# A decoder layer with expert retrieval on one core: PSUM copy for the dots, merged one-hots, a second top-k block in the query stage, and score tiles in three banks

## The chip, the cores and the metric

One core of a Trainium2 chip runs the whole layer. The metric is device time in microseconds (us) of one execution, lower is better. The times are those of the kernel before and of the changed kernel on such a core, and the trace is one profiled execution of each.

## What is computed

One sequence of 1024 tokens of width 1024 in float32 goes through a projection, retention and sliding-window attention, an output projection, a layer norm, and then an expert layer (PEER), whose result is normalised again. The change lies in the expert layer:

```python
q = (xt @ w_pq).reshape(T, H, 2, PEER_HALF)              # H = 8 heads
s = jnp.einsum('thpd,hpkd->thpk', q, sub_keys)           # 128 keys a side
s1, i1 = lax.top_k(s[:, :, 0], K)                        # K = 16
s2, i2 = lax.top_k(s[:, :, 1], K)
cand = (s1[..., :, None] + s2[..., None, :]).reshape(T, H, K * K)
top_s, pos = lax.top_k(cand, K)
idx = jnp.take_along_axis(cand_idx, pos, axis=-1)        # of 16384 experts
g = jax.nn.softmax(top_s, axis=-1)
a = gelu(einsum('cd,ced->ce', xb, u_tab[idx])) * g       # the dots
y = einsum('ce,ced->cd', a, v_tab[idx])
```

## The kernel before, in words

The tokens are eight blocks of 128. Five stages follow one another, each an own block of instructions for the engines, with a barrier between them: `project`, `attend`, `score` (the query stage), `experts_in` and `experts_out`. Float32 products of large matrices are done as three passes over a high and a low part (hi times hi, hi times lo, lo times hi).

The query stage (`score`, from L797 on) has a turn for each of 8 heads: 96 matmuls of 512 columns give the queries, 16 small ones the scores. ScalarE takes the first half of the queries and scores out of PSUM and VectorE the second (`query`, `scores`). The scores of blocks 1 to 7 go to memory; those of block 0 stay (`s_cp`), and VectorE finds their top 16 at the end of the turn of heads 0 to 6: `side` for either side, `pairs` for the sums, and `names` for two heads at a time. Head 7 of block 0 is left to the beginning of `experts_in`.

The expert layer treats the blocks in two ways. For blocks 2 to 7 (768 tokens, `DB` = 6) it multiplies the tokens by all 16384 experts: `experts_in` computes z = u h, 128 tiles of 128 experts, and beside it a dense matrix of gates from one-hots; `experts_out` multiplies gelu(z) times the gates by v. For blocks 0 and 1 (`GB` = 2) it gathers rows: POOL fetches the chosen row of u for 128 tokens with an indirect DMA (`gather`, L1191), and VectorE forms its dot product with the block's tokens (`dot`, L1259), which `h_own` holds in SBUF. There are 2 x 128 = 256 such gathers and dots. They share a ring of three row tiles (`RING` = 3, two gathers ahead): the gather of row i+2 waits until dot i-1 is done (`row_used`).

`experts_in` is laid out by hand in 8 turns of 32 slots. In each slot TensorE does half a tile of z (`z_half`, L1084 to L1086: 24 matmuls of 384 columns). All engines walk through the slots in order, and within a slot in this order:

- TensorE: half a tile, then the gate matmuls (`gates`, 4 small ones, L1094) of the slot before. A tile needs `u_lo` of POOL, and a z bank that ScalarE has read.
- ScalarE: at even slots `u_hi` of the next tile, then the copy of z out of PSUM (L1153) and the store of a whole tile, `scale_hot` (L1125), `take_gates` (L1136), and every 8 steps the store of 2 MB of gates (L1141).
- POOL: at even slots `u_lo` of the next tile (L793), which waits for `u_hi`; then the gathers of the slot. A gather that waits keeps all later work of POOL waiting, `u_lo` too.
- VectorE: the one-hots (`make_hot`, L1248: two instructions of 512 elements a step, which read `near`, a PSUM tile with the numbers 0 to 127, and `iT`), then a piece of the next block's top-k (`top_piece`: three pieces for a head, one for `names`), then the dots of the slot (`own_rows`, from `PER_TURN`).
- SP: u tiles as `u_lo` frees their buffers, the scores for top-k, and in the last turn the first loads of `experts_out` (L1056 z, L1061 and L1069 gates, L1064 v).

Turn s finds the top-k of block s+1, and turns 2 to 7 make the gates of blocks 2 to 7: 32 steps in each, one in a slot, and in turn 7 the same 32 in 21 slots. A step is one make_hot, one scale_hot, one gates and one take_gates, on two sets of buffers in turn. At slot 0 of turns 2 to 7 TensorE transposes the block's `found` and waits for `found_in` (L1107), which VectorE raises at the end of the turn before (L1299). PER_TURN, the dots in the eight turns, is 28, 40, 27, 27, 27, 27, 27, 53.

## Time and profile before

| | before |
|---|---|
| median of 3 runs | 3114.03 us (3112.42 to 3116.70) |
| the profiled execution | 3114.11 us, of which the trace spans 3112.3 us |
| TensorE matmul busy | 2979.0 us, 96% |
| VectorE busy | 2450.3 us, 79% |
| ScalarE, POOL busy | 1191.8 us (38%), 1159.7 us (37%) |
| mean granted TensorE clock | 0.984 |
| chain that ended last | PE 32%, all others 1% or less (the chain covers the last stage) |

The profiler's page says how busy each engine is and which groups of instructions are costliest. A matmul's busy time there overlaps with its neighbour's (they are pipelined), so the time of a run of matmuls is read from their starts in the timeline. A `start us, us` row of the timeline is: start, duration, engine, line, operation, written tile <- read tiles, shapes, and in brackets how long the engine sat idle before and what released it. "SPq", "ACTq" rows are issues of DMAs. The spans of the 8 turns of `experts_in` are found in the timeline as the start of every 768th matmul of L1084 to L1086.

### The profile page before, as it was taken

The page shows a single profiled execution, that of the slowest core. Times are in us where ns is not written, and L with a number is a line of the kernel's source. Part 1 is how long each engine was busy: PE and PEld are TensorE (multiplying, and loading weights), DVE is VectorE, ACT ScalarE, POOL GpSimd, SP SyncE. Part 2 cuts the span into 40 slices and gives each one's busy share as a digit, 9 for nine tenths or more (in the row PEclk, how much of TensorE's full clock was granted, in tenths as well). Part 3 has the DMA queues.
Part 4 walks back from the last instruction along what each step waited for, and adds up shares of the span by engine and source line. Part 5 has one row for each costly group of instructions (what it writes and reads, how often), then busy time and mean ns, then how long its engine had stood idle before and what let it go on. Part 6 is the DMA issues. An engine that isn't in the chain of part 4 may idle for free. (4 is left out here: it accounts for less than half of the span.)

```text
span 3112.3 us, 42565 instructions
## 1 busy us (share of the span) xinstructions
PE 2979.0 (96%) x15866; PEld 2686.6 (86%) x15866; DVE 2450.3 (79%) x4511; ACT 1191.8 (38%) x2213; POOL 1159.7 (37%) x750
## 2 busy tenths in 40 slices
PE   8996998999999999999999999869999999999998
PEld 6886886888999999999999998858888888888887
DVE  4214775455999999999999986569989898999898
ACT  2112332111222466666666656523333333333331
POOL 3222211002656544443444445524434333344331
PEclk9998998999999999999999999989999999999999
DMA  4223222223777666666667677889988888888882
GB/s 172 79 88 132 93 96 82 76 91 114 240 251 255 224 229 239 224 239 243 243 236 240 235 268 280 281 287 314 327 287 307 287 309 307 280 305 297 297 306 78
DMA packets 294024, 695.57 MB, mean 223 GB/s; under 512 B 20432, under 2 KB 136528, under 8 KB 290640
## 3 DMA queue, kind: packets, MB, share of 16 engines
q1 hardware_dynamic: 190928, 316.66, 30.6%
q0 software_dynamic: 73728, 268.47, 25.0%
q10 hardware_dynamic: 29184, 108.01, 9.0%
q8 instruction: 113, 1.85, 0.2%
q14 instruction: 71, 0.58, 0.1%
HBM read 565.13 MB, written 127.93 MB: 223 GB/s over the span
## 5 line engine op out<-in xcount | busy, mean ns | idle before, releaser
L1084 PE MATMUL z_ps<-hT_hi,u_hi 128*128 128x384 f32 x2048 | 703.2, 343 | 18.2 <-POOL u_lo L793 12.7
L1085 PE MATMUL z_ps<-hT_lo,u_hi 128*128 128x384 f32 x2048 | 687.5, 336 | 0.0
L1086 PE MATMUL z_ps<-hT_hi,u_lo 128*128 128x384 f32 x2048 | 687.1, 335 | 0.0
L1393 PE MATMUL y_ps<-v_hi,a_hi 128*128 128x512 f32 x1536 | 600.2, 391 | 24.4 <-DVE y L1521 11.6
L1394 PE MATMUL y_ps<-v_lo,a_hi 128*128 128x512 f32 x1536 | 599.5, 390 | 0.0
L1395 PE MATMUL y_ps<-v_hi,a_lo 128*128 128x512 f32 x1536 | 599.2, 390 | 0.0
L793 POOL TENSOR_TENSOR u_lo<-u_raw,u_hi 128x1024 fp32r<-128x1024 f32 x128 | 315.4, 2464 | 618.2 <-ACT u_hi L789 617.3
L1453 POOL DMA_INDIRECT v_rows<-in_v,room x192 | 286.1, 1490 | 437.8 <-DVE y L1500 414.3
L1084 PEld LDWEIGHTS z_ps<-hT_hi,u_hi 128*128 128x128 f32 x2048 | 387.6, 189 | 20.9 <-POOL u_lo L793 15.3
L1085 PEld LDWEIGHTS z_ps<-hT_lo,u_hi 128*128 128x128 f32 x2048 | 387.6, 189 | 0.0
L1086 PEld LDWEIGHTS z_ps<-hT_hi,u_lo 128*128 128x128 f32 x2048 | 386.6, 189 | 0.0
L1393 PEld LDWEIGHTS y_ps<-v_hi,a_hi 128*128 128x128 f32 x1536 | 289.5, 188 | 85.9 <-issue 12.0
L1394 PEld LDWEIGHTS y_ps<-v_lo,a_hi 128*128 128x128 f32 x1536 | 289.7, 189 | 60.3
L1395 PEld LDWEIGHTS y_ps<-v_hi,a_lo 128*128 128x128 f32 x1536 | 289.5, 188 | 60.2
L1521 DVE TENSOR_TENSOR y<-y_ps,y 128x512 f32<-128x512 f32 x384 | 255.7, 687 | 80.1 <-PE y_ps L1395 77.0
L1259 DVE CUSTOM_DVE_ANT_0 u_rows<-u_rows,h_own 128x1024 f32<-128x1024 f32 x170 | 276.9, 1629 | 46.5 <-DMA u_rows<-in_u,room 34.3
L1153 ACT ACTIVATE z_sb<-z_ps 128x384 f32<-128x384 f32 x256 | 125.8, 491 | 484.1 <-PE z_ps L1086 484.1
L1248 DVE TENSOR_TENSOR hot<-near,iT 128x512 f32<-128x512 f32 x384 | 246.1, 683 | 47.9 <-PE g_ps L1094 47.0
L1125 ACT ACTIVATE hot_g<-hot,gT 128x128 f32<-128x128 f32 x768 | 244.7, 392 | 94.2 <-DVE hot L1248 73.5
L1191 POOL DMA_INDIRECT u_rows<-in_u,room x170 | 208.6, 1227 | 156.3 <-DVE room L1259 132.3
L1500 DVE SCALAR_TENSOR_TENSOR y<-v_rows,a_rows,y 128x1024 f32<-128x1024 f32 x192 | 243.0, 1280 | 4.0 <-DMA v_rows<-in_v,room 3.8
L1421 ACT ACTIVATE v_hi<-room 128x1024 fp32r<-128x1024 f32 x128 | 135.5, 1059 | 276.6 <-DMA room<-in_v 268.9
(189 smaller groups left out, 4818.7 us busy)
## 6 DMA issues: line engine op xcount, KB each, us to landing
u_raw<-in_uT SPq DMA_DIRECT2D x128, 512.0 KB, 3.7
room<-in_v SPq DMA_DIRECT2D x128, 512.0 KB, 6.3
z<-z_sb ACTq DMA_DIRECT2D x128, 384.0 KB, 5.2
gates<-g_sb ACTq DMA_DIRECT2D x24, 2048.0 KB, 8.8
room<-z SPq DMA_DIRECT2D x16, 1536.0 KB, 9.0
z_in<-z SPq DMA_DIRECT2D x16, 1536.0 KB, 8.2
g_in<-gates SPq DMA_DIRECT2D x16, 1536.0 KB, 17.5
room<-gates SPq DMA_DIRECT2D x15, 1536.0 KB, 17.9
```

Of the source, the lines that this page charges most:

```text
L793: self.nc.gpsimd.tensor_tensor(self.u_lo[e][:], self.u_raw[e][:], self.u_hi[e][:].bitcast(F32), ALU.subtract).then_inc(self.u_lo_in[e], 1)
L1084: nc.tensor.matmul(o, u_hi[e][:, k], hT_hi[:, k, cols], start=(k == 0), stop=False)
L1085: nc.tensor.matmul(o, u_hi[e][:, k], hT_lo[:, k, cols], start=False, stop=False)
L1086: last = nc.tensor.matmul(o, u_lo[e][:, k], hT_hi[:, k, cols], start=False, stop=(k == KT - 1))
L1125: last = nc.scalar.activation(hot1_g[g][:, t], hot1[g][:, t], ACT.Copy, scale=gT[:, t0 + t:t0 + t + 1])
L1248: last = nc.vector.tensor_tensor(hot[g][:], bc(iota_ps, 1, 4), bc(iT[:, side, t0:t0 + 4], 2, NK), ALU.is_equal)
L1259: nc.vector.tensor_tensor_reduce(rows_in[r][:], rows_in[r][:], h_own[b][:], 1.0, 0.0, ALU.mult, ALU.add, ahead.z_rows[:, b, slot:slot + 1] ...
L1393: nc.tensor.matmul(o, ah, v_hi[p][:, i, c], start=(i == 0), stop=False)
L1394: nc.tensor.matmul(o, ah, v_lo[p][:, i, c], start=False, stop=False)
L1395: last = nc.tensor.matmul(o, al, v_hi[p][:, i, c], start=False, stop=(i == GROUP - 1))
L1453: nc.gpsimd.indirect_dma_start(out=rows_in[i % RING][:], out_offset=None, in_=d["v"].rearrange("a b c -> (a b) c"), in_offset=bass.Indirec ...
L1521: nc.vector.tensor_tensor(y[:, GB + s, c], y_ps[n % 8][:], y[:, GB + s, c], ALU.add).then_inc(y_read, 1)
```

## The change

Four things change in the expert layer; `UB` is a new constant, equal to `GB`, so that the parts of the diff that treat `UB` > `GB` do nothing here.

1. Dots: one `h_own` of SBUF in place of two, copied by VectorE at the block's first dot into a PSUM tile `h_ps` of two banks, and the dots read that copy.
2. One-hots: the two instructions of `make_hot` become one that writes both (1024 elements).
3. Top-k: in the query stage VectorE finds the top-k of blocks 0 and 1 for heads 0 to 6, one turn later than before. All evacuations of PSUM there go to ScalarE. Head 7 of both blocks, and their gates, come at the beginning of `experts_in`; turn s then treats block s+2, so that turns 6 and 7 have no top-k. The buffers of top-k are doubled. The gathers begin at slot 4 in place of 2 and the dots at slot 6 in place of 4; the dots of the turns are 24, 34, 27, 27, 27, 27, 45, 45.
4. z: a tile's 768 columns are cut into 512 and 256 in place of 384 and 384. The 256 of two tiles share a bank (`z_rest`), so that z needs three banks in place of four and `h_ps` finds room. The second half of a tile now also waits until ScalarE has read the other half of that bank, which is the tile before.

```diff
+UB = 2
+ZB = TB - UB
+ZT = ZB * P
...
-                def query(h, p):
-                    v.wait_ge(q_done, 4 * h + 2 * p + 2)
-                    nc.vector.tensor_copy(qT[p][:, HT:T], q_ps[p][1][:]).then_inc(q_dve, 1)
...
+                def search(h, b):
+                    for p in range(2):
+                        tk.side(link, p, b, h, tk.s_cp[:, b, p])
+                    tk.pairs(link, b, h)
+                    if h % 2:
+                        tk.names(link, b, h // 2)
 
                 def turn(h):
-                    last = h == PH - 1
-                    query(h, 0)
-                    if not last:
+                    if h:
+                        search(h - 1, 0)
+                    if h < PH - 1:
                         split_w(h + 1, 0)
-                    scores(h, 0)
-                    query(h, 1)
-                    if not last:
+                    if h:
+                        search(h - 1, 1)
+                    if h < PH - 1:
                         split_w(h + 1, 1)
-                    scores(h, 1)
-                    v.wait_ge(s_act, 2 * h + 2)
...
+                    v.wait_ge(s_act, 4 * h + 4)
...
-    HT = DT // 2
+    CUT = ZT - 2 * P
...
-    PER_TURN = [28, 40, 27, 27, 27, 27, 27, 53]
+    PER_TURN = [24, 34, 27, 27, 27, 27, 45, 45]
...
-        z_ps = [[bank(f"z_ps{e}{a}") for a in range(2)] for e in range(2)]
+        z_first, z_rest = [bank(f"z_first{e}") for e in range(2)], bank("z_rest")
+        z_ps = [[z_first[e][:, 0:CUT], z_rest[:, e * 2 * P:(e + 1) * 2 * P]] for e in range(2)]
+        h_ps = ctx.enter_context(nc.psum_tensor("h_ps", [P, D], F32))
...
+                def z_half(tile, a):
+
+                    e, i = tile % 2, tile // 2
                     if a == 0:
...
+                        pe.wait_ge(u_lo_in[e], i + 1)
+                        wait(pe, z_read[e], 2 * i)
+                    else:
+                        wait(pe, z_read[1 - e], 2 * ((tile + 1) // 2))
+                    cols = slice(UB * P, UB * P + CUT) if a == 0 else slice(UB * P + CUT, T)
...
+                        if s == 0 and k in (1, 3):
+                            act.wait_ge(gaps, k // 2 + 1)
+                            tk.exp(k // 2).then_inc(exps, 1)
...
-                        if s == 0 and k == 2:
+                        if s == 0 and k == 4:
                             for i in range(EARLY):
                                 gather(i)
...
-                    for hot, side in ((hot2, 1), (hot1, 0)):
-                        last = nc.vector.tensor_tensor(hot[g][:], bc(iota_ps, 1, 4), bc(iT[:, side, t0:t0 + 4], 2, NK),
-                                                       ALU.is_equal)
-                    last.then_inc(hot_in[g], 1)
+                    nc.vector.tensor_tensor(hot[g][:], bc(bc(iota_ps, 1, 4), 1, 2), bc(iT[:, :, t0:t0 + 4], 3, NK),
+                                            ALU.is_equal).then_inc(hot_in[g], 1)
...
+                        v.wait_ge(h_here, 16 * (i // (PH * TOPK) + 1))
+                        link(nc.vector.tensor_copy(h_ps[:], h_own[:]))
+                        nc.vector.engine_nop().then_inc(h_taken, 1)
+                    nc.vector.tensor_tensor_reduce(rows_in[r][:], rows_in[r][:], h_ps[:], 1.0, 0.0, ALU.mult, ALU.add,
                                                    ahead.z_rows[:, b, slot:slot + 1]).then_inc(row_used, 1)
...
+                for b in range(2):
+                    for p in range(2):
+                        tk.side(link, p, b, PH - 1, tk.s_cp[:, b, p])
+                    tk.pairs(link, b, PH - 1)
+                    tk.gaps(b).then_inc(gaps, 1)
+                for b in range(2):
+                    tk.names(link, b, PH // 2 - 1)
+                    v.wait_ge(exps, b + 1)
+                    tk.gates(link, b)
+                    keep_picked(b)
```

## Rows read from the trace of the kernel before

**Rows 1.** Windows: span, busy per engine, clock, DMA share, GB/s; stages and turns.

```profile
531.10:743.80 212.70, 207.21 (x1024) 175.30 (x1024) 93.80 (x249) 34.26 (x48) 2.40 (x1) 0.98 0.25 78
743.80:879.10 135.30, 135.26 (x769) 135.29 (x770) 127.89 (x314) 32.65 (x49) 77.61 (x45) 0.98 0.71 236
879.10:1023.00 143.90, 135.15 (x769) 132.91 (x768) 133.54 (x308) 33.05 (x49) 91.72 (x55) 1.00 0.78 252
1023.00:1189.60 166.60, 163.77 (x1028) 163.45 (x1028) 154.63 (x354) 100.76 (x209) 74.65 (x45) 0.99 0.65 225
1189.60:1351.70 162.10, 162.10 (x1031) 162.07 (x1029) 151.40 (x349) 101.90 (x210) 72.17 (x43) 1.00 0.68 237
...
1837.90:2026.50 188.60, 171.15 (x1029) 167.98 (x1028) 114.79 (x176) 105.14 (x215) 96.94 (x66) 0.96 0.81 287
...
2037.50:3101.30 1063.80, 1050.36 (x4608) 868.26 (x4608) 948.40 (x1185) 340.87 (x504) 391.02 (x262) 0.99 0.84 288
```

**Rows 2.** Waits of TensorE: total us, times, longest.

```profile
PE z_ps L1084 <- POOL u_lo L793: 12.7, 8, 4.0
...
PE g_ps L1094 <- ACT hot_g L1125: 8.9, 4, 3.6
...
PE g_ps L1094 <- ACT g_sb L1136: 4.5, 5, 1.1
PE g_ps L1107 <- DVEq L1299: 2.8, 1, 2.8
```

**Rows 3.** Timeline of TensorE: each row starts 24 matmuls after its partner.

```profile
236.14 0.39 PE L167 MATMUL pp<-w_hi,x_hi 128*128 128x512 f32 x1
...
241.58 0.28 PE L167 MATMUL pp<-w_hi,x_hi 128*128 128x256 f32 x1
...
244.46 0.28 PE L167 MATMUL pp<-w_hi,x_hi 128*128 128x256 f32 x1
...
999.67 0.33 PE L1084 MATMUL z_ps<-hT_hi,u_hi 128*128 128x384 f32 x1
...
1003.83 0.33 PE L1084 MATMUL z_ps<-hT_hi,u_hi 128*128 128x384 f32 x1
```

**Rows 4.** One line's instructions on VectorE: count, duration ns min/median/max.

```profile
L1259 DVE CUSTOM_DVE_ANT_0 u_rows<-u_rows,h_own x170: 1209/1226/3845, 773.1 to 2028.9; 128x1024 f32<-128x1024 f32 x170
...
L1248 DVE TENSOR_TENSOR hot<-near,iT x384: 673/681/693, 1032.4 to 1978.1; 128x512 f32<-128x512 f32 x192
...
L1508 DVE TENSOR_TENSOR z_in<-z_in,g_in x96: 680/686/696, 2071.8 to 3068.4; 128x512 f32<-128x512 f32 x96
```

**Rows 5.** Timeline of VectorE and POOL at the beginning of experts_in (from 743.8).

```profile
750.13 0.29 DVE L742 TENSOR_TENSOR gap<-best 128x128 f32<-128x128 f32 x1
...
755.81 0.29 DVE L767 TENSOR_REDUCE gap_sum<-gap_e 128x8 f32<-128x128 f32 x1 [1.37 <-ACT gap_e L763]
...
759.37 0.29 DVE L724 MAX8 top<-s_in 128x8 f32<-128x128 f32 x1
...
773.21 3.42 POOL L793 TENSOR_TENSOR u_lo<-u_raw,u_hi 128x1024 fp32r<-128x1024 f32 x1 [1.59 <-ACT u_hi L789]
...
774.30 2.37 DVE L749 TENSOR_SCALAR ab<-pos 128x32 uint32<-128x32 uint32 x1
```

**Rows 6.** Timeline of three engines at the beginning of turn 7.

```profile
1839.42 0.33 ACTq L1141 DMA_DIRECT2D gates<-g_sb  x1
...
1845.61 0.94 POOL L1191 DMA_INDIRECT u_rows<-in_u,room  x1 [0.30 <-issue]
...
1854.33 1.22 DVE L1259 CUSTOM_DVE_ANT_0 u_rows<-u_rows,h_own 128x1024 f32<-128x1024 f32 x1 [4.78 <-DMA u_rows<-in_u,room]
```

**Rows 7.** Groups of VectorE in turn 7 (1837.9 to 2026.5): busy, mean, idle before.

```profile
L1259 DVE CUSTOM_DVE_ANT_0 u_rows<-u_rows,h_own 128x1024 f32<-128x1024 f32 x34 | 50.0, 1469 | 35.5 <-DMA u_rows<-in_u,room 34.3
...
L1259 DVE CUSTOM_DVE_ANT_0 room<-room,h_own 128x1024 f32<-128x1024 f32 x18 | 22.7, 1263 | 17.8 <-DMA room<-in_u,room 17.1
```

**Rows 8.** DMA issues of turn 7: count, us from issue to landing.

```profile
u_rows<-in_u,room POOLq DMA_INDIRECT x34, 6.4
```

More of the change, by code:

```diff
@@ L895, in turn @@
                     last = isinstance(h, int) and h == PH - 1
-                    query(h, 0)
+                    query(h, 0, 0)
+                    query(h, 0, 1)
                     if not last:
                         split_w(h + 1, 0)
-                    query(h, 1)
-                    scores(h, 0)
+                    query(h, 1, 0)
+                    for a in range(2):
+                        scores(h, 0, a)
+                    query(h, 1, 1)
                     if not last:
@@ L1149, in _ @@
-                        act.wait_ge(z_done[e], 2 * (2 * m + j) + a + 1)
+                        tile, a = s * SLOTS // 2 + k // 2, k % 2
+                        e, i = tile % 2, tile // 2
+                        if a == 0 and tile < NK - 1:
+                            split_u(tile + 1)
+                        act.wait_ge(z_done[e], 2 * i + a + 1)
                         if a == 0:
-                            wait(act, z_stored[e], 16 * (2 * m + j))
-                        nc.scalar.activation(z_sb[e][:, a * HT:(a + 1) * HT], z_ps[e][a][:, 0:HT],
-                                             ACT.Copy).then_inc(z_read[e], 1)
+                            wait(act, z_stored[e], 16 * i)
@@ L1161, in _ @@
-                        if s < TB - 1 and k == SLOTS - 2:
-                            act.wait_ge(gaps, s + 2)
-                            tk.exp().then_inc(exps, 1)
+                            act.wait_ge(z_read[e], 2 * i + 2)
+                            act.dma_start(d["z"][tile], z_sb[e][:]).then_inc(z_stored[e], 16)
+                        if s == 0 and k in (1, 3):
+                            act.wait_ge(gaps, k // 2 + 1)
+                            tk.exp(k // 2).then_inc(exps, 1)
@@ L1164, in _ @@
+                        if s < TB - 2 and k == SLOTS - 2:
+                            act.wait_ge(gaps, s + 3)
+                            tk.exp(s + 2).then_inc(exps, 1)
+                        if UB > GB and s == TB - 2 and k == SLOTS - 6:
+                            act.wait_ge(row_used, 2 * PH * TOPK)
+                            nc.scalar.activation(kept[:, 2], ahead.z_rows[:, GB], ACT.Gelu).then_inc(late_gelu, 1)
                         for step in steps_at(s, k):
@@ L1291, in _ @@
                             dot(i)
+                        if UB > GB and s == TB - 2 and k == SLOTS - 2:
+                            v.wait_ge(late_gelu, 1)
+                            link(nc.vector.tensor_tensor(kept[:, 2], kept[:, 2], ahead.picked_g[:, GB], ALU.mult))
+                            nc.vector.engine_nop().then_inc(found_in, 1)
                         if s == TB - 1:
-                            for t in range(DB):
+                            for t in range(ZB):
                                 if PRODUCTS_AT[t] == k:
```

308 lines of the change are left out of this document (152 added, 156 removed).

## The prediction

> **What bounds the kernel now.** I read the page first: TensorE is busy 96% of the span. So the only time to be had, as long as TensorE's own work stays the same, is the time in which it stands still or is slowed. Then the windows, one for the query stage, one for each turn of `experts_in` and one for `experts_out` [rows 1]. The turns are the place to look. Turns 3 to 6 take 162.1 us each (one row stands for four), with TensorE busy for all of it: 162.1 is what a turn with 32 gate steps costs when nothing stalls. A turn without gates needs 32 halves of 4.16 us, 133.1 us: 24 matmuls start in 1003.83 - 999.67 = 4.16 us [rows 3]. Against these two floors stand turn 0 with 135.3 (+2.2), turn 1 with 143.9 (+10.8), turn 2 with 166.6 (+4.5) and turn 7 with 188.6 (+26.5) [rows 1]. That is 44 us in all, and the waits of TensorE name their owners: `u_lo` of POOL 12.7 us, the scaled one-hots of ScalarE 8.9, the reading of gates 4.5, `found_in` of VectorE 2.8 [rows 2]. They add up to less than 44 because the wait is followed by a stretch of less than the full clock (mean grant 0.96 in turn 7, 0.99 to 1.00 in turns 2 and 3 [rows 1]), and small gaps inside a step aren't listed.
>
> Behind all of these owners stands VectorE, for two different reasons. In **turn 1** it is full: busy 133.5 us [rows 1], which is as much as TensorE's whole floor of 133.1. Its dots come late, POOL's next gather waits for them in the ring of three, and `u_lo` is queued behind that gather. Turn 2 then begins with the wait for the end of turn 1's top-k. In **turn 7** it isn't full (114.8 of 188.6 us [rows 1]); it sits before the dots and waits for rows: 34.3 + 17.1 us of the turn [rows 7]. A store of 2 MB of gates is issued at 1839.42, a gather at 1845.61, and the dot of that time's rows starts at 1854.33 after 4.78 us of idleness [rows 6]; the one-hots of the next slot stand behind this dot, and TensorE behind the one-hots. A row lands 6.4 us after its issue in the middle [rows 8]; with the dot of 1.3 us and about 1.3 us until POOL issues again, three rows go round in 9 us, 3.0 us a row. Turn 7 asks for 53 rows in 162.1 us, 3.06 us a row. So there is no reserve with which to make good what a burst of transfers costs.
>
> **z in 512 and 256 columns.** 24 matmuls of 512 columns take 241.58 - 236.14 = 5.44 us, 24 of 256 take 244.46 - 241.58 = 2.88 us [rows 3]. Together 8.32 us, as much as 2 x 4.16. Cost 0. Slots are now long and short, 5.44 and 2.88 (with a gate step of (162.1 - 133.1) / 32 = 0.9 us: 6.3 and 3.8). The new wait for `z_read` of the tile before has the long half between, 5.44 us, and stands in TensorE's queue in front of the short half and the gates; ScalarE copies z first thing in its slot, so I take 0, and price a miss under the rivals.
>
> **The dot reads PSUM.** Before, a dot takes 1.226 us in the middle but 3.845 at most [rows 4], and 1.63 in the mean of the page. The one-hots, of which one operand is in PSUM, never take more than 0.693 in 384 [rows 4]. The long ones fall on POOL's `u_lo`: a tensor_scalar of only 32 elements on VectorE took 2.37 at 774.30 while `u_lo` ran from 773.21, and `u_lo` itself took 3.42 [rows 5]. So I price the dot with `h_ps` at 1.23 + 0.08 for reading the sum: 0.4 x 256 = 100 us less on VectorE, of which only what falls into turns 1, 2 and 7 can show. No row shows this instruction with a PSUM operand. Bounds: 1.22 (its minimum, 1.209, is no better) and twice, 2.45. The nearest row is the one-hots', which read PSUM in 0.681 against 0.686 for two SBUF operands of the same size [rows 4], so I take the lower end. The page "SBUF — State Buffer" of the Trainium skill (section "SBUF: two separate sides") says that POOL and a VectorE instruction with two SBUF inputs take a shared pair of ports for a whole instruction each; the trace agrees, 3.845 is about 1.2 plus one `u_lo`. The page "VectorE: DVE Perf Modes" (section on the errata) speaks a little against the change: a PSUM source has a fixed part of 120 cycles against 58, which by its clock would be 0.065 us more a dot, 17 us of VectorE in all; the two rows of equal size don't show it. Two copies of 1024 elements into PSUM, about 1.3 us each, lie in VectorE's queue: under 3 us, covered. The top-k's own two-input instructions can still be held by `u_lo`; I keep 3 to 5 us a turn for them.
>
> **One-hots in one.** Two of 0.681 become one of about 1.23 (the dot's length for 1024 elements): 0.14 x 192 = 26 us less on VectorE, 0.8 us of each pair of slots. TensorE has no wait for it in turns 3 to 6. Cost 0, gain only inside turn 7.
>
> **Top-k of a second block in the query stage.** One head's search takes 750.42 - 743.9 = 6.5 us with `gap`, so 6.2; `names` for two heads ends 1.37 before 755.81, at 754.44, so 4.1 [rows 5]. VectorE is busy 93.8 us of the stage's 212.7 [rows 1]. A turn of a head is 207/8 = 26 us; an odd head's two searches take 2 x (6.2 + 4.1) = 20.6, an even head's 12.4, and the splits of w add 2.4 and the copy 0.3. That fits, and 32 evacuations of 512 elements (some 0.7 us each) have left for ScalarE, which is busy 34.3 us of 212.7 [rows 1]. Splits needed next come between the searches; ahead of the latest stand 10 us of searching and then about 11 us until TensorE needs it. At the stage's end two more copies of 0.6 us run one after the other ahead of the scores' store, which carries 6 blocks in place of 7: +0.5 us. I take +0.5.
>
> **Beginning of experts_in.** VectorE now does two last heads (13), two `names` (8.2), two times gates and the picked numbers (2 x 1.4): it reaches turn 0's first piece about 25 us after the start in place of 15.6 (759.37 - 743.8 [rows 5]). ScalarE's two waits for `gap` come at 10.5 and 18.8 us, when `gap` is there since 6.5 and 13. The gathers wait in POOL's queue ahead of `u_lo`. I follow them: six pieces bring VectorE to 38, `names` to 42, the copy and the first dot to 45; gather 3 waits for it until 45, gather 4 until 48, `u_lo` of tile 6 is then done at 51.5, and TensorE wants it at slot 12, 52 us. A tie: I take 0, and keep 0 to 10 us (each `u_lo` that holds a piece of top-k adds up to 2.4 to VectorE's lateness). VectorE then has 67 + 24 x 1.31 = 98 us of work in turn 0 (67: 8 x 6.2 + 4 x 4.1 and the gates), and catches up.
>
> **Turns 1 and 2.** Turn 1: 67 + 34 x 1.31 + 5 = 117 us against 133.1, in place of 133.5 busy plus waits. `u_lo` isn't held any more: 143.9 becomes 133.3, -10.6. The block of turn 2 has been searched in turn 0, so `found_in` is there and the slower clock behind the wait goes as well: 166.6 becomes 162.3, -4.3.
>
> **Turns 3 to 6.** VectorE falls from 151.4 to about 32 x 1.23 + 67 + 27 x 1.31 + 5 = 147; turn 6 has 45 dots and no top-k, 98. TensorE is on its floor already: 0.
>
> **Turn 7.** 45 rows in 162.1 us are 3.6 us a row, against 3.0 for the ring: a reserve of 0.6 x 8 rows = 5 us between two stores of gates (5.3 slots), which is what a burst takes (4.78 [rows 6]). The turn also begins without a rest of top-k. Of the 26.5 us I let remain what falls to the first burst and to the late loads of gates and v, where no gates slow the slots and rows are asked for every 3.0 us again: 8 us. So 188.6 becomes 170, -18.5. Bounds 0 and -26.5.
>
> **Sum.** +0.5 + 0 - 10.6 - 4.3 - 18.5 = -33 us. `experts_out` (1063.8 us [rows 1]) keeps its work and its loads; VectorE's last dot lies no longer behind the last z store, -1 us. Against the profiled execution, 3114.1 - 34 = 3080 us; that execution stands 0.1 us from the median, so the same holds for it. Own range of this case 3068 to 3090: turn 7 without any stall gives 3072, less the transition's microseconds, and 10 us at the beginning gives 3090.
>
> **Rivals.**
> (a) Turn 7's stalls belong to the transfers, not to the number of rows: DMA share 0.81 at 287 GB/s there against 0.68 and 237 in turn 3 [rows 1]. Each store of gates then still holds a row, whatever the reserve, and only turns 1 and 2 pay: 3114 - 15 = 3099. For it: half of VectorE's idleness is before few rows. Against it: turn 3 to 6 have the same stores and no stall.
> (b) The late beginning: VectorE, held by `u_lo` several times, comes 5 us later than counted, and each pair of slots from 12 to 20 loses 2 us: +10, 3090 with the rest as forecast, 3105 together with (a).
> (c) Slower: the dot on PSUM costs more. Price at 2.45: a turn of 3 to 5 needs 39 + 67 + 27 x 2.53 + 5 = 179 against 162.1, +17 in turns 3 to 5 and +12 in turn 2, turns 0 and 1 (153 and 158 us) +32, turn 7 still -18: about 3190. It turns to a loss where the dot passes (162 - 111) / 27 = 1.9 us, less 0.08. Only the row of the one-hots speaks against it.
> (d) Slower: the short slots. ScalarE's time in a gate step (four scalings of 0.39, 1.1 for the gates, 0.5 for z) no longer fits between long and short halves, in the turn with two steps in a slot above all, and TensorE waits 0.5 us in every second slot of turns 2 to 7: 96 x 0.5 = +48, net 3128. Against it: counted through a pair, ScalarE is ready 1 to 2 us early with one step, and just in time with two.
> (e) Nothing happens: all of the stalls move to another owner. 3110.
>
> **Chances.** Forecast 0.60, (a) 0.17, (b) 0.08, (c) 0.05, (d) 0.05, (e) 0.05. The predicted time is the forecast's. The range, 3068 to 3103, takes in the forecast, (a) and most of (b). A difference under 0.2% (6 us) can hardly be told from none: faster 0.86, within 0.2% 0.05, slower 0.09.
>
> **What would show it.** Windows by turn: turn 1 near 133, turn 2 near 162, turn 7 near 170. Durations of the dot: a maximum near 1.25 in place of 3.85. TensorE's waits: no `u_lo` in turn 1, no L1107's. Starts 24 matmuls apart: 5.44 and 2.88. I am wrong if the dot's median leaves 1.23, if turns 3 to 6 leave 162.1 (short slots), or if turn 0 leaves 135.

## The result and the profile after

The changed kernel took 3082.06 us, median of 4 runs (3081.89 to 3082.50), against 3114.53 us of the kernel before in the same session (4 runs, 3112.42 to 3116.70): a ratio of 0.9896, with a 95% interval of 0.9879 to 0.9913. The forecast was 3080. The profiled execution has a span of 3080.7 us, 31.6 less than the 3112.3 of before.

The windows come first again, cut at the first z matmul of each turn, so that they answer to [rows 1]. Columns: stretch and length, then busy us (and count) of PE, PEld, DVE, ACT and POOL, the granted clock, the DMA share and GB/s. The stretches are the query stage, turns 0, 1, 2, 3, 6 and 7 of `experts_in`, and `experts_out`.

```profile
529.90:741.80 211.90, 206.53 (x1025) 175.36 (x1025) 127.39 (x411) 50.88 (x80) 2.34 (x1) 0.98 0.23 74
741.80:882.70 140.90, 138.09 (x768) 121.38 (x769) 125.39 (x350) 32.47 (x50) 64.06 (x42) 0.97 0.61 214
882.70:1016.10 133.40, 133.40 (x770) 118.07 (x769) 113.16 (x294) 32.90 (x49) 70.89 (x50) 1.00 0.71 249
1016.10:1179.10 163.00, 163.00 (x1030) 147.08 (x1028) 138.91 (x314) 100.21 (x209) 67.01 (x44) 1.00 0.64 228
1179.10:1342.10 163.00, 163.00 (x1029) 147.05 (x1029) 139.97 (x317) 101.41 (x210) 66.24 (x43) 1.00 0.66 236
1668.10:1831.10 163.00, 163.00 (x1030) 147.07 (x1029) 94.85 (x131) 101.33 (x209) 81.29 (x62) 1.00 0.79 284
1831.10:1998.80 167.70, 164.84 (x1030) 147.89 (x1028) 93.15 (x127) 105.60 (x216) 77.18 (x59) 1.00 0.84 306
2006.20:3069.70 1063.50, 1050.18 (x4608) 868.00 (x4607) 947.70 (x1185) 339.36 (x503) 356.03 (x261) 0.99 0.84 288
```

Set against the forecast, stretch by stretch, in us. The times are differences of the starts of every 768th z matmul, so they have two decimals; the windows above round them. The last z matmul is counted to turn 7 with 0.34 us. `experts_out` is taken from its first matmul's start to its last one's end (the last window above begins 0.4 us late).

| stretch | before | after | change | forecast |
|---|---|---|---|---|
| stages ahead of the query stage | 531.1 | 530.2 | -0.9 | none |
| query stage, to the first z matmul | 212.7 | 211.5 | -1.2 | +0.5 |
| turn 0 | 135.24 | 140.94 | +5.7 | 0 (0 to +10) |
| turn 1 | 143.93 | 133.44 | -10.5 | -10.6 |
| turn 2 | 166.61 | 162.93 | -3.7 | -4.3 |
| turns 3 to 6 | 4 x 162.06 | 4 x 163.01 | +3.8 | 0 |
| turn 7 | 188.65 | 167.64 | -21.0 | -18.5 |
| last z matmul to first of `experts_out` | 10.98 | 7.02 | -4.0 | -1 |
| `experts_out` | 1063.8 | 1063.9 | +0.1 | 0 |

They add up to -31.7, the difference of the spans but for rounding. The sum of the forecast was -34, so the total is close, but three terms are off by 3 to 6 us each and offset one another. The experiments are about these.

TensorE's waits from 700 to 2100 us (engine and line that waits, what it waits for, total us, times, longest), which answer to [rows 2]; two of `experts_out` are left out:

```profile
PE y_ps L1443 <- DVE a_lo L1564: 7.1, 1, 7.1
PE z_first L1104 <- PEq L825: 5.1, 1, 5.1
PE z_first L1104 <- POOL u_lo L799: 4.5, 2, 2.8
...
PE g_ps L1114 <- ACT g_sb L1157: 1.0, 1, 1.0
```

`u_lo` has gone from 12.7 us in 8 waits to 4.5 in 2, the scaled one-hots (8.9) are off the list, and so is the wait behind the top-k at a turn's beginning (2.8).

The dots, one line's instructions (count, ns min/median/max, first and last start), which answer to [rows 4]:

```profile
L1285 DVE CUSTOM_DVE_ANT_0 u_rows<-u_rows,h_ps x170: 1209/1221/1224, 792.5 to 1999.3; 128x1024 f32<-128x1024 f32 x170
L1285 DVE CUSTOM_DVE_ANT_0 room<-room,h_ps x86: 1209/1221/1223, 789.6 to 2000.7; 128x1024 f32<-128x1024 f32 x86
```

The longest of 256 dots is 1.224 us, where it was 3.845. Rival (c), a dearer dot, is out with that. The first dot also starts 20 us later than before (789.6 against 769.2).

### The profile page after: what moved, and what is told of

Read it like the earlier page. It is cut to its first block and busy times, and to the rows that moved or that the text cites. A ratio compares the mean times of both kernels' runs of the same rounds, so it can differ in the third digit from the quotient of the medians.

```text
span 3080.7 us, 42384 instructions
## 1 busy us (share of the span) xinstructions
PE 2980.4 (97%) x15866; PEld 2565.9 (83%) x15866; DVE 2327.8 (76%) x4289; ACT 1204.8 (39%) x2245; POOL 1053.0 (34%) x750
## 5 line engine op out<-in xcount | busy, mean ns | idle before, releaser
L1443 PE MATMUL y_ps<-v_hi,a_hi 128*128 128x512 f32 x1536 | 600.1, 391 | 20.4 <-DVE y L1572 11.5
L1104 PE MATMUL z_first<-hT_hi,u_hi 128*128 128x512 f32 x1024 | 409.9, 400 | 9.5 <-PEq L825 5.1
L1106 PE MATMUL z_first<-hT_hi,u_lo 128*128 128x512 f32 x1024 | 401.3, 392 | 0.0
L1105 PE MATMUL z_first<-hT_lo,u_hi 128*128 128x512 f32 x1024 | 400.7, 391 | 0.0
L1273 DVE TENSOR_TENSOR hot<-near,iT 128x1024 f32<-128x1024 f32 x192 | 234.1, 1222 | 124.2 <-PE g_ps L1114 122.2
L1104 PE MATMUL z_rest<-hT_hi,u_hi 128*128 128x256 f32 x1024 | 297.0, 290 | 0.0
L1105 PE MATMUL z_rest<-hT_lo,u_hi 128*128 128x256 f32 x1024 | 289.7, 283 | 0.0
L1106 PE MATMUL z_rest<-hT_hi,u_lo 128*128 128x256 f32 x1024 | 289.6, 283 | 0.0
L1285 DVE CUSTOM_DVE_ANT_0 u_rows<-u_rows,h_ps 128x1024 f32<-128x1024 f32 x170 | 207.3, 1219 | 73.7 <-DMA u_rows<-in_u,room 62.0
L1104 PEld LDWEIGHTS z_first<-hT_hi,u_hi 128*128 128x128 f32 x1024 | 193.7, 189 | 46.4 <-issue 5.2
L1106 PEld LDWEIGHTS z_first<-hT_hi,u_lo 128*128 128x128 f32 x1024 | 193.3, 189 | 42.5
```

The costliest lines, as they stand in the source:

```text
L1104: nc.tensor.matmul(o, u_hi[e][:, k], hT_hi[:, k, cols], start=(k == 0), stop=False)
L1105: nc.tensor.matmul(o, u_hi[e][:, k], hT_lo[:, k, cols], start=False, stop=False)
L1106: last = nc.tensor.matmul(o, u_lo[e][:, k], hT_hi[:, k, cols], start=False, stop=(k == KT - 1))
L1273: nc.vector.tensor_tensor(hot[g][:], bc(bc(iota_ps, 1, 4), 1, 2), bc(iT[:, :, t0:t0 + 4], 3, NK), ALU.is_equal).then_inc(hot_in[g], 1)
L1443: nc.tensor.matmul(o, ah, v_hi[p][:, i, c], start=(i == 0), stop=False)
```

## The experiments

The stretches of all profiled executions stand together here; each run's edit and verdict follow. `transition` is the stretch between the last z matmul and the first of `experts_out`. Each span is of one execution.

| kernel | turn 0 | turn 1 | turn 2 | turn 3 | turn 6 | turn 7 | transition | span |
|---|---|---|---|---|---|---|---|---|
| before | 135.24 | 143.93 | 166.61 | 162.06 | 162.07 | 188.65 | 10.98 | 3112.3 |
| after | 140.94 | 133.44 | 162.93 | 163.03 | 163.01 | 167.64 | 7.02 | 3080.7 |
| after, dots on SBUF | 141.96 | 133.44 | 162.91 | 163.01 | 165.85 | 176.06 | 11.52 | 3097.6 |
| before, z split | 135.47 | 144.78 | 164.88 | 163.11 | 163.14 | 189.92 | 10.38 | 3113.8 |
| before, z split, PSUM dots | 135.49 | 133.44 | 163.08 | 163.16 | 163.18 | 179.97 | 6.57 | 3086.6 |
| after, 53 rows in turn 7 | 141.00 | 133.44 | 162.91 | 163.03 | 163.01 | 177.77 | 6.67 | 3088.7 |
| after, two one-hots | 141.79 | 133.44 | 163.06 | 163.15 | 163.10 | 169.07 | 6.59 | 3081.6 |
| after, u loads first | 141.73 | 133.44 | 162.92 | 163.02 | 163.03 | 168.40 | 6.29 | 3081.0 |
| after, 384/384 and iota in SBUF | 140.46 | 133.12 | 162.67 | 162.76 | 164.86 | 174.49 | 7.09 | 3086.4 |
| u loads first, ring of 4 | 141.70 | 133.44 | 162.94 | 163.03 | 163.03 | 164.71 | 6.25 | 3077.3 |
| the same, dots from slot 12 | 136.14 | 133.44 | 162.92 | 163.06 | 163.02 | 164.33 | 6.25 | 3072.1 |
| after, again | 140.88 | 133.44 | 162.91 | 163.02 | 163.02 | 167.15 | 7.01 | 3077.5 |

The stretches hardly scatter: turn 1 is 133.44 in every kernel with z split and its stall gone, and the changed kernel's turn 7 came out at 167.64 and 167.15. So differences of half a microsecond can be read from single executions in turns 1 to 5. In turns 0 and 7 something under 1 us isn't safe: the order of SP's loads alone moved turn 7 by 0.8 (experiment 6). Those of spans can't be read so finely: the stages ahead of the query stage, which no edit here touches, vary from 527.0 to 531.7.

**1. Is it the place of the dot's operand?** The changed kernel, whose dots read the block from SBUF again, one tile for each of the two blocks; the copy into PSUM is still made. To find room, one small tile moves into free space of another, and one that nothing uses here goes.

```diff
-        h_own = sb("h_own", [P, D])
+        h_own = [sb(f"h_own{b}", [P, D]) for b in range(2)]
...
-                    nc.vector.tensor_tensor_reduce(rows_in[r][:], rows_in[r][:], h_ps[:], 1.0, 0.0, ALU.mult, ALU.add,
+                    nc.vector.tensor_tensor_reduce(rows_in[r][:], rows_in[r][:], h_own[b][:], 1.0, 0.0, ALU.mult, ALU.add,
```

> The changed kernel with one thing undone: the dots read the block's tokens from SBUF again (both blocks have a tile of their own there; the copy into PSUM is still made, and not read; two small tiles are placed elsewhere to make room). Theory 1 (what the changed kernel gains in turn 1 comes from any relief of VectorE, in turn 7 from fewer rows): the dot's mean goes back to about 1.6 us with a maximum near 3.8, turn 1 needs 67 + 34 x 1.7 + 5 = 130 us of VectorE, just under 133, and shows 133 to 136; turn 7 stays at 168 to 173; in all 3082 to 3092 us. Theory 2 (the length of the dot alone is the gain): turn 1 goes back to about 144 and turn 7 to about 185, in all about 3110.

One run, 3099.42 us; before on that chip 3115.61. The dots' row:

```profile
L1285 DVE CUSTOM_DVE_ANT_0 u_rows<-u_rows,h_own x170: 1209/1226/3848, 793.3 to 2013.4; 128x1024 f32<-128x1024 f32 x170
```

The long dots are back (3.848; each of the 57 over 1.5 us runs beside a `u_lo`), and 17 us with them, nearly all in three places: turn 7 (+8.4), turn 6 (+2.8) and the transition (+4.5). So it is the operand's place; in size the result lies between the two theories. Turn 1 isn't among the three:

```profile
884.20:1017.60 133.40, 133.40 (x770) 118.07 (x770) 123.52 (x295) 32.92 (x49) 85.95 (x49) 1.00 0.76 249
```

It holds the search of a block and no one-hots, as before; with 34 dots in place of 40 VectorE is busy 123.5 us in place of 133.5, which leaves enough slack for dots on SBUF too.

**2. and 3. The split of z alone, then with the dots on PSUM.** Both start from the kernel before. The first has only the 512/256 split with its banks and its added wait:

```diff
-        z_ps = [[bank(f"z_ps{e}{a}") for a in range(2)] for e in range(2)]
+        CUT = DT - 2 * P
+        z_first, z_rest = [bank(f"z_first{e}") for e in range(2)], bank("z_rest")
+        z_ps = [[z_first[e][:, 0:CUT], z_rest[:, e * 2 * P:(e + 1) * 2 * P]] for e in range(2)]
...
+                    else:
+                        wait(pe, z_read[1 - e], 2 * ((4 * m + n // 2 + 1) // 2))
```

> The kernel before with one part of the change alone: z in 512 and 256 columns in three banks. Theory 1 (the split itself costs TensorE 0.02 us a tile, and some more beside gates): turns 3 to 6 at 163.0 instead of 162.1, turns 1 and 7 as before at about 144 and 189; in all about 3114 + 6 = 3120. Theory 2 (the 0.9 us that turns 3 to 6 of the changed kernel have lost come from the merged one-hots or from ScalarE, not from the split): 162.1 in turns 3 to 6, in all 3114.

The second adds the copy and the dots on it; top-k, row counts and one-hots stay those of before:

```diff
+                    if slot == 0:
+                        link(nc.vector.tensor_copy(h_ps[:], h_own[b][:]))
+                    nc.vector.tensor_tensor_reduce(rows_in[r][:], rows_in[r][:], h_ps[:], 1.0, 0.0, ALU.mult, ALU.add,
```

> The kernel before with the split of z and the dots on a PSUM copy, and nothing else: 28, 40, 27, ... 53 dots, top-k and one-hots as before. Theory 1: turn 1 needs 67 + 40 x 1.31 + 5 = 125 us of VectorE and runs at 133.4, turn 2 at 163; turn 7 still asks for 53 rows, 3.06 us a row against the ring's 3.0, and keeps its stalls, 185 to 190; in all about 3120 - 15 = 3105. Theory 2 (the long dots were what held up turn 7 as well): turn 7 at 168 to 172, in all about 3087.

One run each: 3115.58 and 3088.38 us, before on that chip 3115.61. Windows of the split alone (turns 1, 3 and 7, columns as above):

```profile
877.40:1022.10 144.70, 136.62 (x770) 119.54 (x769) 133.73 (x308) 32.88 (x49) 89.69 (x55) 0.99 0.77 250
...
1187.00:1350.10 163.10, 163.05 (x1029) 147.07 (x1028) 148.62 (x349) 101.54 (x210) 70.37 (x43) 1.00 0.66 236
...
1839.60:2029.50 189.90, 172.27 (x1030) 152.75 (x1028) 114.53 (x179) 105.52 (x215) 101.75 (x67) 0.96 0.80 288
```

and of the split with PSUM dots (turns 1 and 7):

```profile
876.90:1010.30 133.40, 133.40 (x770) 118.06 (x769) 116.81 (x305) 32.97 (x49) 77.95 (x55) 1.00 0.79 271
...
1826.10:2006.10 180.00, 169.66 (x1030) 151.02 (x1028) 108.47 (x181) 105.79 (x216) 85.38 (x67) 0.97 0.85 306
```

Two things follow. First, a turn of 32 gate steps costs 163.1 in both, as in the changed kernel, and 162.06 before: the split alone costs 1.0 us a turn. The total doesn't show it (3115.58 against 3115.61, where 3120 was expected), as turn 2 and the stages ahead came out 1.7 us shorter each. Second, the dots on PSUM by themselves are worth 3113.8 - 3086.6 = 27 us: turn 1 falls to its floor with 40 dots, turn 2 to 163.1 with its block still searched in turn 1, turn 7 by 10.0 and the transition by 3.8. In turn 7 VectorE is busy 6.1 us less and POOL 16.4 us less. The total is that of theory 2, but turn 7 lies between the theories (180.0). Taken out of the changed kernel the same edit costs 17 us (experiment 1), since the other edits then cover part of its gain, turn 1's above all.

**4. 53 rows in turn 7.** The changed kernel with the rows of before in its last two turns.

```diff
-    PER_TURN = [24, 34, 27, 27, 27, 27, 45, 45]
+    PER_TURN = [24, 34, 27, 27, 27, 27, 37, 53]
```

> The changed kernel with 37 and 53 dots in turns 6 and 7 instead of 45 and 45. Theory 1 (the ring of three rows has no reserve at 53): turn 7 goes from 167.7 back to 185 to 190 us, and experts_out begins later behind the last dot (11 instead of 7 us after TensorE's last z): in all about 3104. Theory 2 (the number of rows doesn't matter, the shorter dots and one-hots do): turn 7 stays at 168 to 170, in all 3082 to 3084.

One run, 3090.53 us, between the theories; only turn 7 moved, 167.6 to 177.8. With the others that gives turn 7 by rows and by the dot's operand. The cells of 53 rows with SBUF dots and with PSUM dots are experiments 2 and 3, whose one-hots are still two, and whose top-k is still that of before; experiment 4 has one.

| turn 7, us | 53 rows | 45 rows |
|---|---|---|
| dots on SBUF | 189.9 (two one-hots) | 176.1 |
| dots on PSUM | 180.0 (two), 177.8 (one) | 167.6 |

Eight rows fewer are worth 10.1 us, the operand's place 8.4 to 10.0. The 2.2 us between 180.0 and 177.8 are the merged one-hots and the moved top-k together.

Where do the 10.1 us lie? TensorE's slots say it. With 53 rows slot 3 takes 7.32 us in place of 4.79, slot 11 5.88 in place of 4.93, slot 21 8.95 in place of 6.23, and slots 27 and 28 take 7.20 and 6.92 in place of 4.69 and 5.57; the others agree within 0.1. Each of these long stretches comes 17 to 23 us behind the issue of a store of gates (1.8, 47.6, 105.5 and 137.0 us into the turn), and one store (78.4) has none. In the kernel before, four rows issued from 0.2 us ahead of the store at 1839.42 to 10.4 behind it landed after 9.0 to 11.4 us, against 6.4 in the middle [rows 8]. So by their timing the stores start the stalls (no run leaves a store out), and the number of rows decides how much of one reaches TensorE. TensorE's waits in turn 7 with 53 rows (those with 45 are `u_lo` 1.7 and `g_sb` 1.0):

```profile
PE z_first L1104 <- POOL u_lo L799: 4.2, 1, 4.2
PE g_ps L1114 <- ACT hot_g L1146: 3.2, 2, 2.0
```

The granted clock has a part in it too. Two stretches of 3.4 us of that turn have the lower clock (0.50, which is 1.2 in place of 2.4 GHz), each from about the end of one of these waits on, and the turn with 45 rows has none. Before, there were four, of which one row:

```profile
1908.80:1912.20 3.40, 3.39 (x13) 3.40 (x14) 2.65 (x7) 2.23 (x6) 1.86 (x2) 0.50 0.65 196
```

At half speed 3.4 us do the work of 1.7; so by an estimate from these rows the lower clock made up at most 4 x 1.7 = 6.8 of the 26.5 us that turn 7 lost before.

Now VectorE. Its groups in turn 7 of the changed kernel (busy, mean ns | idle before, what ended it), which answer to [rows 7]:

```profile
L1285 DVE CUSTOM_DVE_ANT_0 u_rows<-u_rows,h_ps 128x1024 f32<-128x1024 f32 x29 | 35.3, 1218 | 21.7 <-DMA u_rows<-in_u,room 21.1
L1285 DVE CUSTOM_DVE_ANT_0 room<-room,h_ps 128x1024 f32<-128x1024 f32 x15 | 18.2, 1216 | 20.4 <-DMA room<-in_u,room 20.3
```

Over the whole turn it waits 41.4 us for rows in 44 dots (0.94 a dot), with 53 rows 54.9 in 53 (1.04), and before 51.4 in 52 (0.99 [rows 7]). That looks as if nothing but the number had changed. But the one-hots, on which TensorE's gate steps depend, end with slot 20, and one single wait behind them, 13.7 us long, is a third of the 41.4. VectorE's waits in slots 0 to 20 alone, with 45 rows (1831.1 to 1946.8 us):

```profile
DVE hot L1273 <- PE g_ps L1114: 28.0, 12, 5.1
DVE u_rows L1285 <- DMA u_rows<-in_u,room: 14.9, 8, 4.2
...
DVE room L1285 <- DMA room<-in_u,room: 2.0, 3, 0.8
```

and with 53 rows (1830.1 to 1949.3 us):

```profile
DVE u_rows L1285 <- DMA u_rows<-in_u,room: 18.5, 11, 5.2
DVE hot L1273 <- PE g_ps L1114: 14.1, 7, 3.9
DVE room L1285 <- DMA room<-in_u,room: 12.1, 5, 5.1
```

There the wait for rows falls from 30.6 to 16.9 us with eight rows fewer in the turn, and VectorE's wait for TensorE, which is its lead, rises from 14.1 to 28.0.

**5. Two one-hots again.** The changed kernel with the two instructions of before in place of the one.

> The changed kernel with the one-hots of a step in two instructions of 512 elements again. Theory 1 (the merge matters only where VectorE is late): turns 3 to 6 stay at 163.0 us, turn 7 goes from 167.6 to about 170, the difference between the two earlier runs with 53 rows (180.0 with two instructions, 177.8 with one); in all about 3084. Theory 2 (the one long instruction delays ScalarE and is the cause of the 0.9 us that turns 3 to 6 lost): they go back to 162.1, in all about 3080.

One run, 3083.44 us (before on that chip 3113.76). Turn 7 takes 169.07 against 167.64 and 167.15, the gate turns 163.15 against 163.0. The merged one-hots are worth 0.1 us in each turn with gates before the last and some 1.4 to 1.9 in turn 7, which is hardly more than turn 7 moves without them (168.40 in experiment 6); and they aren't where turns 3 to 6 got their 1.0 us.

**6. Turn 0: u loads ahead of the scores' load.** The timelines of the changed kernel in turn 0 (start, length, engine, line, instruction; idle before it and what ended it), of VectorE, SP's queue, ScalarE, POOL and TensorE in this order:

```profile
763.82 3.37 DVE L762 TENSOR_TENSOR room<-room,top_i 128x512 f32<-128x512 f32 x2
...
773.29 0.33 SPq L1059 DMA_DIRECT2D s_in<-scores  x1
773.66 0.91 SPq L1064 DMA_DIRECT2D u_raw<-in_uT  x2
...
777.36 1.06 ACT L795 ACTIVATE u_hi<-u_raw 128x1024 fp32r<-128x1024 f32 x1 [7.18 <-DMA u_raw<-in_uT]
...
778.50 2.35 POOL L799 TENSOR_TENSOR u_lo<-u_raw,u_hi 128x1024 fp32r<-128x1024 f32 x1 [9.62 <-ACT u_hi L795]
...
780.90 0.50 PE L1104 MATMUL z_first<-hT_hi,u_hi 128*128 128x512 f32 x1 [2.81 <-POOL u_lo L799]
```

The load of the next scores waits until VectorE has taken the last ones. It stands in SP's queue ahead of two u tiles, goes out at 773.29, and the u tiles leave only behind it, at 773.66 and 774.14. That is 32 us after the first z matmul. Before, they left 19.4 and 23.5 us after it (763.21 and 767.33, merged in one row):

```profile
763.21 4.45 SPq L1050 DMA_DIRECT2D u_raw<-in_uT  x2
```

ScalarE waits 7.18 us, POOL 9.62, and TensorE's slots 7 and 8 take 5.84 and 7.19 us where their like take 2.87 and 5.47. VectorE itself is later than before mainly by the second block's work, which the forecast counted, and some 3 us later than forecast; its own two-operand instructions are held while `u_lo` runs: the two of L762 took 3.37 us together, 2.77 of it the first. So the edit turns the order round:

```diff
+                        for e in range(2):
+                            if 2 * m + j:
+                                sp.wait_ge(u_lo_in[e], 2 * m + j)
+                                sp.dma_start(u_raw[e][:], d["uT"][4 * m + 2 * j + e]).then_inc(u_here[e], 16)
                         if m < Q * (TB - 2):
                             wait(sp, s_taken[j], m)
```

> The changed kernel with one order swapped in SP's queue of experts_in: the loads of the u tiles stand before the load of the scores, which waits for VectorE. Theory 1 (turn 0 lost its 5 us because u tile 4 was issued only when VectorE had freed the scores' buffer): turn 0 goes from 140.9 to about 136, nothing else moves; in all about 3077. Theory 2 (POOL's gathers, which wait for the late first dots, hold u_lo anyway): the stall only moves from slot 7 to about slot 12 and turn 0 stays at 138 to 141, in all 3080 to 3082.

One run, 3082.82 us. Turn 0 takes 141.7, no less. The second of those u loads now leaves at 766.67, but the stall has moved to slots 11 and 12 (6.59 and 7.19 us), where POOL's queue makes it:

```profile
780.77 2.39 POOL L799 TENSOR_TENSOR u_lo<-u_raw,u_hi 128x1024 fp32r<-128x1024 f32 x1 [4.84 <-ACT u_hi L795]
792.76 0.96 POOL L1215 DMA_INDIRECT room<-in_u,room  x1 [9.60 <-DVE room L1285]
...
796.56 2.36 POOL L799 TENSOR_TENSOR u_lo<-u_raw,u_hi 128x1024 fp32r<-128x1024 f32 x1
```

The gather at 792.76 has waited 9.60 us for the first dot, and `u_lo` is behind it. This is rival (b), which the first stall had hidden: of two late queues only the later one shows.

**7. 384/384 with the iota in SBUF.** The banks and the cut of before in the changed kernel; the room that this takes in PSUM comes from the one-hots' iota, which they read from SBUF then.

```diff
-    CUT = ZT - 2 * P
+    CUT = ZT // 2
...
-        iota_ps = near[:, 0:NK]
+        iota_ps = iota[:]
```

> The changed kernel with z in 384 and 384 columns and four banks again; the bank comes from the numbers 0 to 127, which the one-hots now read from SBUF. Theory 1 (the split costs 0.3 us in a turn without gates and 1.0 with): turns 3 to 6 at 162.1 us, turn 1 at 133.1; the one-hots can be held by u_lo and go from 1.22 to about 1.6 in the mean, which VectorE can bear in turns 3 to 6 (158 of 162), and which costs turn 7 some 3 us; in all about 3079. Theory 2 (VectorE has no room for it): turns 3 to 5 go over 163 and turn 7 over 175, in all over 3085.

One run, 3088.22 us. Turn 1 takes 133.12, 0.3 less than with the split. The gate turns (162.7 to 163.2) aren't a clean reading of it, as waits of 7.7 us for ScalarE's `g_sb` have come in. The one-hots are:

```profile
L1269 DVE TENSOR_TENSOR hot<-iota,iT 128x1024 f32<-128x1024 f32 x192 | 280.3, 1463 | 65.2 <-PE g_ps L1111 64.5
```

against 1222 ns in the changed kernel, where the longest takes 1.226 us and here 3.427. An ordinary tensor_tensor is held like the dot once both operands are in SBUF, and turn 7 takes 6.9 us more. Theory 2 has the total; turns 3 to 5 stayed at 162.7 to 163.2.

**8. A ring of four rows.** Experiment 6 with one more row in flight.

```diff
-    RING, EARLY = 3, 2
+    RING, EARLY = 4, 3
```

> The changed kernel with the u tiles first in SP's queue, and in experts_in a ring of four rows with three gathers ahead instead of three and two (two small tiles are placed elsewhere for the room). Theory 1 (three rows in flight are too few for a burst of transfers): turn 7 goes from 167.6 to about 164, in all 3 to 4 us below the run with the swapped order alone, about 3073. Theory 2 (what is left in turn 7 belongs to the transfers and the two-step slots): turn 7 stays at 167 to 168, in all about 3077.

One run, 3079.09 us, against 3082.82 of experiment 6 on the same chip. Turn 7 falls from 168.40 to 164.71. The groups of its dots:

```profile
L1285 DVE CUSTOM_DVE_ANT_0 u_rows<-u_rows,h_ps 128x1024 f32<-128x1024 f32 x34 | 41.4, 1216 | 9.9 <-DMA u_rows<-in_u,room 8.1
L1285 DVE CUSTOM_DVE_ANT_0 room<-room,h_ps 128x1024 f32<-128x1024 f32 x11 | 13.4, 1216 | 13.3 <-DMA room<-in_u,room 12.9
```

Waiting for rows takes 21.0 us where it took 50.9 in experiment 6 (27.4 + 23.5), and in slots 0 to 20 VectorE doesn't wait for a row at all (39.3 us for TensorE). The turn is 1.7 above a turn 3 to 6, but only 0.4 above turn 7 in experiment 9, where TensorE has no wait in it.

**9. and 10. Dots of turn 0 from slot 12, beside the changed kernel.** The last stall of turn 0 is the gather that waits for the first dot. So the kernel of experiment 8 asks for no dots before slot 12; the number of rows stays.

```diff
-            first = 6 if s == 0 else 0
+            first = 12 if s == 0 else 0
```

> The run with the u tiles first in SP's queue and four rows in the ring, and on top the dots of turn 0 from slot 12 on instead of slot 6 (24 dots in 20 slots). Theory 1 (the whole stall of turn 0 is VectorE's late arrival, caught first by SP's queue and, where that is mended, by POOL's gather that waits for the first dot): VectorE reaches slot 12 some 56 us after the start, POOL's first waiting gather comes at slot 14, 60 us; turn 0 goes from 141.7 to about 136, turn 1 stays at 133.4, turn 7 at 164.7, in all about 3074. Theory 2 (the bunched dots of turn 0 only move the wait once more): turn 0 stays over 139, in all 3077 to 3079.

> The changed kernel as it is, beside the run before on the same chip: 3082 us, turn 0 at 141, turns 3 to 6 at 163.0, turn 7 at 167.6. Every theory expects this; it is there for the difference to the run before.

Both were timed four times on one chip, against 3115.81 us of before (3113.96 to 3122.25). The version took 3074.41 us (3071.43 to 3075.79), ratio 0.9861 (0.9843 to 0.9879); the changed kernel 3080.91 (3079.25 to 3082.42), ratio 0.9885 (0.9867 to 0.9902). The intervals of the ratios overlap a little; the eight times themselves don't, and the profile names the places. Turn 0 and turn 7 of the version, columns as above:

```profile
742.80:878.90 136.10, 136.10 (x768) 120.04 (x769) 125.80 (x349) 32.72 (x50) 65.72 (x42) 0.98 0.63 221
...
1827.40:1991.70 164.30, 164.25 (x1030) 147.78 (x1028) 95.70 (x132) 105.38 (x216) 75.87 (x58) 1.00 0.84 310
```

From the first z matmul to the end the version takes 3072.1 - 742.8 = 2329.3 us, the changed kernel 3077.5 - 738.6 = 2338.9: 9.6 us, 4.7 in turn 0, 2.8 in turn 7, 0.8 in the transition and 1.3 in `experts_out`. The medians differ by 6.5 only; in the profiled executions the stages ahead, where the two are alike, took 4.7 us longer in the version (531.7 against 527.0).

## Why the prediction was right, and where it was not

**The dot on PSUM: right.** Forecast 1.23 + 0.08, measured 1.22; the 0.08 for reading the sum lies within it, as the next instruction starts together with that reading. The nearest row, the one-hots with one PSUM operand, told the price. The relief was 94 us and not the 100 of the forecast: its mean of 1.63 is that of 170 of the dots, and all 256 had 1.585, now 1.219. The Trainium skill, "SBUF — State Buffer", section "SBUF: two separate sides", says that a VectorE instruction with two SBUF inputs and a POOL instruction that reads SBUF exclude each other. Experiments 1 and 7 agree: the dot goes back to 3.848 at most, and the one-hots from 1.222 to 1.463 in the mean. The forecast's estimate from the Trainium skill's "VectorE: DVE Perf Modes" (section on the errata) would have made each dot 0.065 us longer for its PSUM source; its median went from 1.226 to 1.221, so nothing of that shows.

**Turns 1 and 2: right in size, too simple in cause.** -10.5 and -3.7 against -10.6 and -4.3. The forecast credited the operand's place together with fewer dots and the moved search. Either is enough: turn 1 is 133.44 with SBUF dots and 34 rows, and 133.44 with PSUM dots and 40 rows. Turn 2 misses its 162.3 only by what the split costs.

**Turn 7: right in size, its mechanism only half of it.** The forecast gave all of its -18.5 to the ring: 45 rows leave a reserve of 0.6 us a row, from which bursts are made good. That part is as it said, but worth about 10 us: with 53 rows in the changed kernel the stalls behind four of the turn's five stores of gates come back or grow, and VectorE's waits for TensorE, its lead, are half as long (experiment 4). As much again came from what the sum held at nothing here, the operand's place (8.4 to 10.0 us in turn 7), with a share of the one-hots that hardly stands clear. The forecast's cycle of the ring took 1.3 us for a dot; in turn 7 before, the dots took 1.47 and 1.26 in the mean [rows 7], and now 1.22. What of the 8.4 to 10.0 us is the shorter dot and what is POOL's earlier next gather was not separated. Nor were the first burst and the late loads, for which 8 us were left, what remained: slot 3 has no stall any more, the changed turn 7 is 3.3 us above that of experiment 9, and this sits in slots 21, 27 and 28. Rival (a), that the transfers alone decide and rows don't, is refuted by experiment 4, though by their timing it is the transfers that start each stall.

**The split of z: the term 0 was wrong.** It costs 0.3 us in a turn without gates (experiment 7) and 1.0 in a turn with them (experiment 2), that is 1.0 + 4 x 1.0 + about 1 for turns 2 to 7, and 0.3 each for turns 0 and 1: some 6 to 7 us. The rows were read too coarsely. In [rows 3] 512 and 256 columns together match twice 384 to the last digit shown, but in turn 1 of the changed kernel (timeline of TensorE, 48 matmuls apart)

```profile
999.70 0.40 PE L1105 MATMUL z_first<-hT_lo,u_hi 128*128 128x512 f32 x1
...
1008.04 0.40 PE L1105 MATMUL z_first<-hT_lo,u_hi 128*128 128x512 f32 x1
```

a pair takes 8.34 us where 8.32 was counted, and 16 pairs make the 0.3. Small differences per slot have to be read over a whole turn. Why gate steps add 0.7 more is open: no wait longer than those listed stands in turns 3 to 6. In turn 3 the starts inside the halves account for 0.4 of the 1.0 us; the piece from a long half's last start to the next z matmul, with its gate step, takes 0.055 us more than before, and that behind a short half 0.024 less, 16 times each. Rival (d), 0.5 us in every second slot, was 8 times too high.

**Turn 0: the term 0 was wrong, the range held it.** The failed step is the one that followed only POOL's queue. The change makes VectorE take the scores later, and three queues hang on that, of which SP's, with the u tiles behind the scores' load, breaks first. The working followed the gathers and not the loads of the same loop. VectorE also reached turn 0's first piece 28.1 us after the start (769.84), not 25: the pair of L762, once for each block, took 3.4 us each time beside `u_lo`. The tie at slot 12 that the forecast spoke of was real, though: experiment 6 shows it as 5 to 6 us, experiment 9 takes it away.

**Query stage: sign wrong, size small.** Forecast +0.5. It takes 212.5 to 212.7 us in the three kernels without the second block's search and 210.6 to 211.6 in the nine with it, so the move brings about 1.3 us; why was not looked into.

**Transition: mis-sized.** Forecast -1, measured -4.0. TensorE doesn't wait for the z store there but for VectorE, whose last dots and product end after the last z matmul. Before, the wait was

```profile
PE y_ps L1393 <- DVE a_lo L1513: 11.0, 1, 11.0
```

and the last dot ended 7.1 us after the last z matmul, now 3.2: the same 4 us. The end of turn 7 in the changed kernel (timeline of VectorE, with one row each of ScalarE and TensorE):

```profile
1999.31 1.21 DVE L1285 CUSTOM_DVE_ANT_0 u_rows<-u_rows,h_ps 128x1024 f32<-128x1024 f32 x1
...
2001.83 0.69 DVE L1295 TENSOR_TENSOR room<-room 128x512 f32<-128x512 f32 x1
2002.81 1.06 ACT L1475 ACTIVATE v_hi<-room 128x1024 fp32r<-128x1024 f32 x1 [3.69 <-PEq L1047]
2003.90 1.23 DVE L1577 TENSOR_TENSOR v_lo<-room,v_hi 128x1024 fp32r<-128x1024 f32 x1 [1.39 <-ACT v_hi L1475]
2005.05 0.68 DVE L1564 TENSOR_TENSOR a_lo<-room,a_hi 128x512 fp32r<-128x512 f32 x1
...
2005.78 0.80 PE L1443 MATMUL y_ps<-v_hi,a_hi 128*128 128x512 f32 x1 [7.08 <-DVE a_lo L1564]
```

The last product ends at 2002.5. Only behind it does `experts_out` begin on ScalarE (the barrier between the stages), and `v_hi`, then `v_lo` and `a_lo`, hold TensorE until 2005.78. With PSUM dots the transition is 6.3 to 7.1 us in every kernel, even with 53 rows; with SBUF dots it is 10.4 to 11.5.

**The rivals' sums.** (b) together with (a) was put at 3105; from the forecast's own terms it is 3099 + 10 = 3109, which lies outside the range that it gave. The result didn't come near it.

So the total was right in part by luck, because errors cancelled: +5.7 us in turn 0 and +4.5 in turns 1 to 6 of unforeseen cost against -2.5, -3 and -1.7 us of unforeseen gain in turn 7, the transition and the query stage, and -0.9 in stages that the change doesn't touch.

## What to carry to other kernels

When two engines hold each other up, try moving one operand of the longer instruction to the other memory before moving work between engines. Here this one edit gave 27 us alone, and is still worth 17 of the 32 us beside the others: gains in the same slack don't add, so an edit's worth depends on what stands beside it. When a change makes one engine later in its order, follow every queue that waits for it, loads included, and not only the one that already hurt: a stall that is mended uncovers the next, as turn 0 showed. When a ring of buffers paces an engine, count the waits only where the bottleneck hangs on them: over the whole turn the wait per dot had hardly fallen, in the slots with one-hots the waits had gone from 30.6 to 16.9 us. And look for the slots in which the bottleneck stands still before explaining an average.
